# Six of TensorE's meetings passed without waiting, and the next stage's first tile taken part by part

## What is computed

```python
# first block
hn = rms_norm(h, ln_pre_mix);  proj = hn @ w_in          # queries, keys, values of two attentions
h = h + rms_norm(concat(sliding_window(...), forgetting(...)) @ w_out, ln_post_mix)
hn = rms_norm(h, ln_pre_ffn);  gu = hn @ w_gate_up       # 2 x 2816 columns
h = h + rms_norm((silu(gu[:, :D_FF]) * gu[:, D_FF:]) @ w_down, ln_post_ffn)

# second block
h = rmsnorm(x, norm1);  proj = h @ w_in                  # a_q a_k a_v | a_gate b_f b_i b_q b_gate g_a g_b
o_a = rmsnorm(gated_delta_rule(...), a_onorm) * silu(a_gate);      y_a = o_a @ w_branch_a
o_b = rmsnorm(hgrn2_recurrence(...), b_onorm) * sigmoid(b_gate);   y_b = o_b @ w_branch_b
mix = sigmoid(g_a) * y_a + sigmoid(g_b) * y_b
x = x + mix @ w_out
x = x + peer(rmsnorm(x, norm2))      # 128 experts per token, gathered by index
return rmsnorm(x, final_norm)
```

## Time and profile before

| | |
|---|---|
| median of 3 runs | 3375.86 us (3374.03 to 3380.77) |
| the execution that was profiled | 3369.78 us |
| its span, first to last instruction | 3368.0 us |
| PE busy | 2824.0 us (84% of the span) |
| DVE, ACT, POOL busy | 1806.6, 918.1, 1068.8 us |
| mean granted clock of TensorE | 0.936 |

### The profile page before, as it was taken

One profiled execution on the slowest core, in us unless ns is written; L12 is line 12 of the kernel. 1 busy time (PEld: TensorE's weight loads), 2 busy tenths in 40 slices (PEclk: granted clock), 3 DMA queues, 4 the chain that ended last, 5 costly groups with the idle time before them and its releaser, 6 DMA issues.

```text
span 3368.0 us, 32768 instructions
## 1 busy us (share of the span) xinstructions
PE 2824.0 (84%) x11178; PEld 1867.2 (55%) x11178; DVE 1806.6 (54%) x3673; ACT 918.1 (27%) x1517; POOL 1068.8 (32%) x722
## 2 busy tenths in 40 slices
PE   5988899998998988999789987777777777777776
PEld 3866588785667976779767663333333333333332
DVE  1056233303666633239633237777777777777765
ACT  3244422223655134233543321111111111111100
POOL 2300244441000002345233334444444444444342
PEclk9999999998998999999999989998998899999999
DMA  3200122222110001221112229999999999999998
GB/s 118 78 20 1 51 94 93 87 100 106 69 63 13 1 26 63 88 94 45 63 69 86 90 106 413 396 396 395 408 396 396 401 412 396 398 398 407 401 400 341
DMA packets 115300, 671.68 MB, mean 199 GB/s; under 512 B 16232, under 2 KB 17512, under 8 KB 49008
## 3 DMA queue, kind: packets, MB, share of 16 engines
q0 software_dynamic: 73728, 536.90, 38.9%
q1 hardware_dynamic: 31536, 114.83, 9.6%
q10 hardware_dynamic: 9920, 18.42, 1.6%
HBM read 663.78 MB, written 6.32 MB: 199 GB/s over the span
## 4 chain that ended last, share of the span: by engine, by line
PE 44%; issue 24%; DMA 14%; DVE 13%; ACT 3%; POOL 2%; DVEq 0%; ACTq 0%; PEldq 0%; POOLq 0%; PEld 0%
PE ps L930 14%; DMA arena<-in_experts,arena 13%; PE ps L399 8%; PE ps L400 8%; PE ps L401 8%; POOL ring_r L1962 2%; DVE arena L1938 1%; PE ps L565 1%; DVE arena L1790 1%; PE ps L537 1%; PE ps L456 1%; DVE arena L1943 1%; DVE arena L1789 1%; DVE arena L1772 1%; PE ps L563 1%
## 5 line engine op out<-in xcount | busy, mean ns | idle before, releaser
L930 PE MATMUL ps<-arena 128*128 128x512 f32 x2048 | 979.5, 632 | 319.6 <-DVE arena L1943 319.5
L1962 POOL TENSOR_TENSOR ring_r<-ring,w_hi 128x1024 fp32r<-128x1024 f32 x191 | 470.2, 2462 | 1422.9 <-ACT w_hi L956 1299.0
L930 PEld LDWEIGHTS ps<-arena 128*128 128x128 f32 x2048 | 399.9, 202 | 892.6 <-DVE arena L1943 447.5
L2000 POOL DMA_INDIRECT arena<-in_experts,arena x512 | 556.5, 1087 | 793.5 <-PE ps L930 737.6
L1938 DVE SCALAR_TENSOR_TENSOR arena<-arena,ring 128x1024 f32<-128x1024 f32 x512 | 618.9, 1224 | 265.9 <-DMA arena<-in_experts,arena 237.6
L399 PE MATMUL ps<-n_hi,w_hi 128*128 128x512 f32 (+1 forms) x1264 | 503.5, 398 | 50.6 <-DVE low L1441 20.5
L401 PE MATMUL ps<-n_hi,ring_r 128*128 128x512 f32 (+1 forms) x1264 | 493.6, 391 | 0.0
L956 ACT ACTIVATE w_hi<-ring 128x1024 fp32r<-128x1024 f32 x175 | 185.1, 1058 | 651.2 <-PE ps L401 642.2
L400 PE MATMUL ps<-slot_r,w_hi 128*128 128x512 f32 x896 | 359.1, 401 | 0.0
L1412 ACT ACTIVATE hgel<-hdot 128x2 f32<-128x2 f32 x256 | 52.0, 203 | 1109.2 <-DVE arena L1938 1109.2
L399 PEld LDWEIGHTS ps<-n_hi,w_hi 128*128 128x128 f32 x1264 | 240.6, 190 | 132.1 <-issue 50.8
(11 more groups left out here) (322 smaller groups left out, 3758.4 us busy)
## 6 DMA issues: line engine op xcount, KB each, us to landing
ring<-in_weights SPq DMA_DIRECT2D x215, 512.0 KB, 3.5
arena<-in_experts,arena POOLq DMA_INDIRECT x512, 12.5
arena<-low_rest ACTq DMA_DIRECT2D x2, 2048.0 KB, 10.4
h_all<-in_xT ACTq DMA_DIRECT2D x1, 2112.0 KB, 16.4
h_rest<-h_all ACTq DMA_DIRECT2D x1, 2048.0 KB, 7.5
low_rest<-slot_r ACTq DMA_DIRECT2D x1, 2048.0 KB, 7.4
h_all<-h_rest ACTq DMA_DIRECT2D x1, 2048.0 KB, 8.6
out<-w_hi_f SPq DMA_DIRECT2D x4, 512.0 KB, 7.6
```

The costliest lines, as they stand in the source:

```text
L930: last = mm(ps[:, yb + half, :], diag[:, j, :], uv[:, j, D + half * 512:D + half * 512 + 512], start=False, stop=False)
L1962: g_.tensor_tensor(ring_r[:, n % RING], ring[:, n % RING], w_hi[:, n % PAIR].bitcast(F32), ALU.subtract).then_inc(w_ready, 1)
L2000: g_.indirect_dma_start(uv[:, n % UV, :], None, experts, bass.IndirectOffsetOnAxis(ap=idxu[:, n // PAIRS, e:e + 1], axis=0)).then_inc(uv_i ...
```

## The change

On PE the meetings 1, 5, 11, 12, 16 and 17 become `through(n)`: PE drains and increments `phase` as before, so that the others can meet, but doesn't wait. ACT and DVE meet as before. In place of the wait:

- 1: PE waits for `f_act` at 1 there, and for the meeting (`phase` at 3) only in `spread_negcum(0)`.
- 5: PE waits for `ff_done` at 21 and, in the first tile of `down`, for `norm_ready` before each of the 22 parts.
- 11, 16 and 17: the next `project` is called with `fresh` set, so its first tile waits for `norm_ready` part by part.
- 12: nothing.

On DVE the last instruction of each part now increments `norm_ready` (22 in `gated_unit`, and 8 for each of the three stages), and ACT's wait for that semaphore in the next stage is raised by 22.

```diff
--- before.py
+++ after.py
@@ -377,6 +377,10 @@
             mm, tr = nc.tensor.matmul, nc.tensor.transpose
             count = {"chunk": 0, "evac": 0, "sq": 0, "norm": 0, "link": 0}
 
+            def through(n):
+
+                pe.drain().then_inc(phase, 1)
+
             def take():
                 n = count["chunk"]
                 count["chunk"] += 1
@@ -493,10 +497,13 @@
                 last.then_inc(f_ready, 1)
 
             project(13, (n_hi, low1), L, True, forget_logits, 2, QUERIES)
-            meet(pe, 1)
+            through(1)
+            pe.wait_ge(f_act, 1)
 
             def spread_negcum(n):
 
+                if n == 0:
+                    pe.wait_ge(phase, 3 * 1)
                 for u in ((0, 1), (2, 3), (4,), (5,), (6,), (7, 8))[n]:
                     if u >= 2:
                         pe.wait_ge(neg_taken, u - 1)
@@ -600,12 +607,16 @@
                                      [x[:, k, META:L] for x in (n_hi, low1)], k == 0, k == DT - 1)
                     last.then_inc(chunk_done, 1)
             count["chunk"] += 2 * FT - 4
-            meet(pe, 5)
+            through(5)
+            pe.wait_ge(ff_done, FT - 1)
             for m in range(DT):
                 b = banks()
                 for c in range(DOWN_CH):
                     w = take()
                     for k in range(c * DT, min(c * DT + DT, FT)):
+                        if m == 0:
+                            count["norm"] += 1
+                            pe.wait_ge(norm_ready, count["norm"])
                         last = three(ps[:, b, :], [p[:, k - c * DT, :] for p in w],
                                      [x[:, k, META:L] for x in (ff_hi, ff_lo)], k == 0, k == FT - 1)
                     last.then_inc(chunk_done, 1)
@@ -794,10 +805,10 @@
             sum_chunk(4, NC - 1)
             meet(pe, 10)
             project(8, (hi2, parts(7)), SEQ, True)
-            meet(pe, 11)
-            project(8, (parts(3), parts(4)), SEQ)
+            through(11)
+            project(8, (parts(3), parts(4)), SEQ, True)
             project(8, (hi2, parts(7)), SEQ)
-            meet(pe, 12)
+            through(12)
 
             project(16, (hi2, parts(7)), SEQ)
             meet(pe, 13)
@@ -872,11 +883,11 @@
             sum_chunk(4 + NC, NC - 1)
             meet(pe, 15)
             project(8, (hi2, parts(6)), SEQ, True)
-            meet(pe, 16)
-            project(8, (parts(5), parts(3)), SEQ)
+            through(16)
+            project(8, (parts(5), parts(3)), SEQ, True)
             project(8, (hi2, parts(6)), SEQ)
-            meet(pe, 17)
-            project(8, (parts(2), parts(1)), SEQ, False, sums_behind(n_all[:, :, META:L]))
+            through(17)
+            project(8, (parts(2), parts(1)), SEQ, True, sums_behind(n_all[:, :, META:L]))
             def key_scores(n):
 
                 t, part = n // PARTS, n % PARTS
@@ -1149,7 +1160,7 @@
             hi2 = n_hi[:, :, META:L]
             for k in range(DT):
                 split(tokens(2)[:, k, :], hi2[:, k, :])
-            act.wait_ge(norm_ready, 4 * DT)
+            act.wait_ge(norm_ready, 4 * DT + FT)
             act.dma_start(low_rest.ap(), tokens_low).then_inc(low_moved, 16)
             dst3 = [tokens(0), tokens(1), tokens(2)]
             normr = region(B[3], 8, SEQ)
@@ -1554,7 +1565,8 @@
                 dve.wait_ge(ff_done, gated_at)
                 v.tensor_scalar(ff_hi[:, m, META:L], ff[:, m, META:L], 1.0, None, ALU.mult).then_inc(ff_upper, 1)
                 dve.wait_ge(ff_upper, gated_at)
-                v.tensor_tensor(ff_lo[:, m, META:L], ff[:, m, META:L], ff_hi[:, m, META:L].bitcast(F32), ALU.subtract)
+                v.tensor_tensor(ff_lo[:, m, META:L], ff[:, m, META:L], ff_hi[:, m, META:L].bitcast(F32), ALU.subtract
+                                ).then_inc(norm_ready, 1)
 
             for j in range(2):
                 gated_unit(j, slice(j, j + 1), j + 1, c0 + 2 * j + 2)
@@ -1731,8 +1743,8 @@
             for n in range(8):
                 v.tensor_tensor(OA[:, n, :], OA[:, n, :], gate("a_gate", n), ALU.mult).then_inc(evac, 1)
                 if n >= 1:
-                    lower(OA[:, n - 1, :], parts(3)[:, n - 1, :], parts(4)[:, n - 1, :])
-            lower(OA[:, 7, :], parts(3)[:, 7, :], parts(4)[:, 7, :])
+                    lower(OA[:, n - 1, :], parts(3)[:, n - 1, :], parts(4)[:, n - 1, :]).then_inc(norm_ready, 1)
+            lower(OA[:, 7, :], parts(3)[:, 7, :], parts(4)[:, 7, :]).then_inc(norm_ready, 1)
             meet(dve, 11)
             YA, MX = tokens(0), tokens(1)
             for n in range(8):
@@ -1830,16 +1842,16 @@
             for n in range(8):
                 v.tensor_tensor(OBt[:, n, :], OBt[:, n, :], gate("b_gate", n), ALU.mult).then_inc(evac, 1)
                 if n >= 1:
-                    lower(OBt[:, n - 1, :], parts(5)[:, n - 1, :], parts(3)[:, n - 1, :])
-            lower(OBt[:, 7, :], parts(5)[:, 7, :], parts(3)[:, 7, :])
+                    lower(OBt[:, n - 1, :], parts(5)[:, n - 1, :], parts(3)[:, n - 1, :]).then_inc(norm_ready, 1)
+            lower(OBt[:, 7, :], parts(5)[:, 7, :], parts(3)[:, 7, :]).then_inc(norm_ready, 1)
             meet(dve, 16)
             for n in range(8):
                 g_ = gate("g_b", n)
                 link(v.tensor_tensor(g_, YA[:, n, :], g_, ALU.mult))
                 v.tensor_tensor(MX[:, n, :], MX[:, n, :], g_, ALU.add).then_inc(evac, 1)
                 if n >= 1:
-                    lower(MX[:, n - 1, :], parts(2)[:, n - 1, :], parts(1)[:, n - 1, :])
-            lower(MX[:, 7, :], parts(2)[:, 7, :], parts(1)[:, 7, :])
+                    lower(MX[:, n - 1, :], parts(2)[:, n - 1, :], parts(1)[:, n - 1, :]).then_inc(norm_ready, 1)
+            lower(MX[:, 7, :], parts(2)[:, 7, :], parts(1)[:, 7, :]).then_inc(norm_ready, 1)
             dve.wait_ge(h_moved, 32)
             meet(dve, 17)
             for n in range(8):
```

## The result

| | before | changed |
|---|---|---|
| median | 3374.95 us (3373.55 to 3380.77, 4 runs) | 3342.62 us (3339.68 to 3346.06, 4 runs) |
| the execution that was profiled | 3369.78 us | 3343.43 us |
| its span | 3368.0 us | 3341.6 us |
| mean granted clock | 0.936 | 0.939 |

The ratio is 0.9902 with an interval from 0.9888 to 0.9916: 33.1 us of 3374.95 less (28.3 to 37.8). The forecast was 3343 with 32.7 less. One execution of all those that this document rests on, of the kernel that asks for all parts at once, took 4687.82 us at a mean granted clock of 0.554 and is left out of that kernel's ratio; every other one lies within 0.3% of its kernel's median.

What follows compares the result with a forecast made beforehand. PE was taken to set the pace, interrupted by meetings and the slow clock behind them. Gains 6.96 + 6.41 + 7.61 + 6.49 + 5.24 + 0 = 32.7 us, off the median 3375.86, gave 3343; range 3333 to 3360.

Steps and rivals of the forecast that it cites:

- What bounded the kernel: PE's five waits at `meet`, 26.4 us together, and lowered clock in the five first tiles behind them, 9.81 us.
- Meetings 11, 16, 17: PE starts on ready parts, only part 7 (0.70 us) remains after the old start: gains 6.96, 6.41 and 7.61 us.
- Meetings 5 and 12: Nothing is waited for, PE goes on after its drain at full clock: gains 5.24 and 6.49 us.
- the bound of 0.72: At the passed meetings, PE's drain was taken at 0.36 us, between 0 and twice that, 0.72.
- Meeting 1: Gain 0 (between -0.1 and +0.1 us): the next tile waits by `evac` for the same ACT copy.
- What is added: 46 waits on `norm_ready` at PE's matmuls, as many DVE increments, and ACT's threshold: cost taken as 0, at most 3.7 us.
- What is late next: Behind the passed meetings, weight chunks stay in time: chunk 2 takes 3.6 us against PE's 5.6, with 2.0 to spare.
- The clock falls all the same: Rival: all five first tiles keep their old time behind the drain, gain 24.6 us, 3351; chance 0.09.
- The weights take the meeting's place: Rival: rounding and subtraction for chunk 2 come late, 1.81 us five times, gain 23.6 us, 3352; chance 0.06.
- It doesn't do what it says: Rival: another wait of the first tile holds PE until the meeting is over, 3376; chance 0.04.
- Slower: Rival: dense PE work from meeting 10 to 13 makes the chip lower the clock behind 11, 3433; chance 0.03.
- The sum: Five gains and meeting 1's 0 give 32.7 us, passing through to the end: 3343 by the median.

Runs made afterwards that it cites:

- the kernel that asks for all parts at once: Changed kernel, but at 11, 16 and 17 PE waits for all eight parts before the first matmul: 0.9968 of before, 10.8 us less.
- clock alone: Kernel before, all meetings kept, PE multiplying constants into an unused bank while waiting at 5, 11, 12, 16 and 17: 0.9971, 9.8 us less.
- 5 and 12 alone: Kernel before with only meetings 5 and 12 passed by PE, with the part waits of down's first tile: 0.9962, 12.8 us less.
- the constants at 19: Changed kernel with ACT's last two loads of constants, placing and final_norm, issued two stages earlier, behind the keys: 0.9877 of before, 3330.76 us.
- the three edits: Changed kernel with DVE's lower half directly behind its product, no PE drain at passed meetings, constants loaded early: 0.9862 of before, 3326.64 us; repetition 0.9870.
- the kernel that took the other engine away: Kernel with all three edits, plus DVE instead of GpSimd making the second weight chunk's lower half behind 11, 16 and 17: 0.9869 of before, 3326.68 us.

## Why the prediction was right, point by point

**What bounded the kernel.** The five waits of the earlier trace rows and the slow tiles behind them were the reachable time. The parts measured apart fit together: clock alone 9.8 (forecast 9.81 from the windows), 5 and 12 alone 12.8 (11.73), the parts at 11, 16 and 17 22.3 (20.98). The last two differ from their forecasts by about 1.2 us, which their intervals (8.8 us wide for the first) don't resolve; in the traces the terms are right to 0.15 each. That agreement tests one side only: each term is what stood in the profile of before, read off, less what was forecast to be left. The part read off moves with the clock from one execution to the next. The first tile behind 17 took 8.31 us there, but 7.02 and 7.05 in the two other profiles in which PE is idle for 6.3 us ahead of it (5 and 12 alone, all parts at once).

**Meetings 11, 16, 17.** Gains 6.83, 6.27, 7.48 against 6.96, 6.41, 7.61: each 0.13 or 0.14 too high. Part 7 was the one that counts, which the kernel with part 6 moved ahead shows, and the working placed PE's start on it right. The 0.13 are two things, at 11 for example. Part 7's first matmul starts 6.05 us behind the last one of the old stage instead of 6.00 (1317.65 to 1323.70, before 1321.39 to 1327.39), as DVE's last product takes 2.50 us instead of 2.45. And from there to the 25th it takes 0.78 us, not 0.70: behind a wait the next matmul starts 0.32 us later, not 0.23 (1323.70 to 1324.02). The same delay behind the wait for part 6 (1322.90 to 1323.23) costs nothing, since part 7 is waited for all the same. The idle time before part 6 at 17 was 0.98 (forecast 0.9).

**Meetings 5 and 12.** 5.21 and 6.57 against 5.24 and 6.49. The drain, taken at 0.36, left idle times of 0.26 to 0.39, and costs 0.63 and 0.49 us where nothing hides it, by the kernel without it; the bound of 0.72 held.

**Meeting 1.** 0, and the wait for ACT's copy is the same 2.52 us; the faster clock behind it is not the change's.

**What is added.** The 46 waits cost nothing where they are met: the first tile at 5, which has them, takes 5.63 us, that at 12, which has none, 5.66, both behind a drain. The tile of the earlier trace rows with 5.63 has eight such waits as well, as the prediction says.

**What is late next.** Nothing in the second or third tiles: the two waits for `ring_r` are those of before, and the weights' transfers now run during the first tiles (DMA share 0.23 to 0.31). The lower half of chunk 2 is ready at 1328.29, and PE starts that tile at 1329.92, so 1.6 of the forecast 2.0 us were to spare.

**The rivals.** *The clock falls all the same*: no, 1.00 in all five. Pauses of 0.2 to 1.0 us, one or two a stage, didn't lower it. But the two rows at 1.00 that the prediction set against this rival were one execution's luck: behind the same two waits, of 2.61 to 2.65 and of 1.81 or 1.82 us, the clock is lowered in three and in two of the eleven profiles (see the last section). What speaks against the rival is the pauses left, shorter than those: none of them lowered the clock in any of the profiles that have them. The rule of the Trainium skill that the prediction cited for this rival (TensorE: Matmul & The Clock Gate, section "A second HAM failure mode: psum-queue depth-cycling") speaks of frequent pauses; no trace here shows such a case. *The weights take the meeting's place*: no. *It doesn't do what it says*: true of meeting 1 alone; the kernel that asks for all parts at once shows what it would have been at the other three. *Slower*: no, 82.5 us behind the first tile of meeting 11 and 50 us behind meeting 12 at 1.00.

**The sum.** 32.36 in the traces, 33.1 by the ratio, 32.7 in the forecast. That the median, 3342.62, lies 0.4 us from the forecast 3343 is luck: the gain is known to 4.7 us either way, and the four runs spread over 6.4. That the gain goes through to the end holds within the interval; the forecast's reason, that each later stage starts from PE's tiles, isn't tested by itself, but the same size came through with two meetings, with five, and with the constants at 19 (10.1 us of idle time and 0.9 of slow clock in the trace, 8.4 by the ratios).

**The best kernel.** The one with the three edits, 0.9862 and 0.9870 in two measurements, some 1.3 to 1.4% below before and some 11 to 14 us below the changed kernel; most of it is meeting 19's constants (0.9877 when added to the changed kernel by themselves).

## What to carry to other kernels

A meeting of engines costs the waiting one its idle time and the slow tile behind it; read both, then ask who comes last and which part of the next operand that is, since a meeting often only names the wait for data (0.02 us of 5.61 were the meeting's own here). Where the consumer takes its first tile part by part, only the last part's lateness remains, and moving any earlier part brings nothing. Where the wait has to stay, work without a purpose in it keeps the clock (10 us for 48 matmuls in the trace here), and where an engine comes last because of a load, its issue can often go ahead of the stage.

## What was not expected of the hardware

**The same idle time, with and without a fall of the clock.** In all eleven profiles PE is idle for 1.99 us ahead of the output projection of the first block. In four the tile behind it, counted to the start of the 25th matmul, takes 5.63 or 5.64 us (340.19 in the kernel before is one), in five 8.26 to 8.33 with a first matmul of 0.76 or 0.77, and in two the clock is low for a part of it only (6.92 and 7.19). It is not the program: the kernel with the three edits, profiled twice, shows both. PE in order of time in its first profile, and in its second:

```profile
343.68 0.76 PE L403 MATMUL ps<-n_hi,w_hi 128*128 128x512 f32 x1 [1.99 <-DVE mix_lo L1451]
```

```profile
339.44 0.47 PE L403 MATMUL ps<-n_hi,w_hi 128*128 128x512 f32 x1 [1.99 <-DVE mix_lo L1451]
```

The stretches from there to the start of the 25th matmul, again of the first profile and of the second:

```profile
343.68:351.95 8.27, 8.27 (x25) 0.65 0.01 2
```

```profile
339.44:345.08 5.64, 5.63 (x24) 1.00 0.01 3
```

Three other waits between these two lengths behave alike. The 2.52 us ahead of the values' projection are followed by a lowered clock in five of the eleven profiles, the 2.61 to 2.65 us at 70 us in three, and the 1.81 or 1.82 us ahead of the tile that starts at 1482.73 in the kernel before in two. The worst of them, in the first profile with the three edits, where the kernel before has 1.00:

```profile
70.12:78.82 8.70, 8.70 (x25) 0.64 0.05 18
```

After the idle times of 4.25 to 6.34 us at the five starts it fell in every profile that has them; after the short ones inside the first tiles, up to 1.6 us with the three edits, it didn't. So for a wait of 1.8 to 2.7 us the price is open by up to 2.9 us from one execution to the next, and a single profile doesn't tell it.

**A product of 0.69 us that takes 2.5** beside another engine's subtraction, at every tile of these stages. It stands in the earlier trace rows as a plain duration of 2.45, and only the kernel that took the other engine away showed that most of it isn't work. The other engine's row stands in the earlier trace rows: it ends at 1325.38, and the product 0.55 us behind it, at 1325.93.
